# Sending the tenth weight chunk directly behind the ninth, in a hybrid decoder step with a mixture of 32 experts

## The reference, cut to what matters

```python
def decoder_layer(x, start, past_k, past_v, past_u, w):
    ...
    x = x + merged @ w['w_out']
    hn = rms_norm(x, w['norm_ffn_g']).reshape(B * S, D_MODEL)
    x = x + hier_moe(hn, ...).reshape(B, S, D_MODEL)

def hier_moe(h, ...):
    # top-1 of 4 groups, then top-2 of its 8 experts for every token
    ...
    def expert_block(args):
        xb, e = args
        return (jax.nn.silu(xb @ w_gate[e]) * (xb @ w_up[e])) @ w_down[e]
```

## Time and profile before

| | |
|---|---|
| median of three runs | 1030.26 us (1027.77 to 1032.42) |
| the profiled execution's own time | 1030.08 us |
| its span, first to last instruction | 1028.2 us |
| TensorE busy | 903.1 us (88%) |
| DVE, ACT, GpSimd busy | 365.2, 224.2, 85.4 us |
| moved by the DMA engines | 258.46 MB, mean 251 GB/s |
| DMA rate from about 540 us to about 1000 us | 385 to 413 GB/s |

### The profile page before, as it was taken

The page is one execution under the profiler, slowest core; times in us unless marked ns, Lnnn a source line. Parts: engine busy times, 40 slices in busy tenths (PEclk is TensorE's granted clock), DMA queues, the critical chain, the costliest instruction groups (busy, mean ns, idle before and its releaser), DMA issues.

```text
span 1028.2 us, 11181 instructions
## 1 busy us (share of the span) xinstructions
PE 903.1 (88%) x4299; PEld 507.0 (49%) x4299; DVE 365.2 (36%) x806; ACT 224.2 (22%) x570; POOL 85.4 (8%) x88
## 2 busy tenths in 40 slices
PE   6899799999899999999969999797777778887884
PEld 5454577777678888855533333233232323232331
DVE  4588568767343345533334111111011111111110
ACT  3432354254632100022211111001000000000010
POOL 0100000000000000000011211011111111010111
PEclk9999899999999999999969999899999999989998
DMA  9621212111112227088389999999999999999991
GB/s 316 202 82 71 93 42 81 51 42 58 66 42 82 83 82 263 15 346 339 144 301 400 395 388 393 390 411 397 400 401 403 410 398 413 403 413 396 405 393 44
DMA packets 33327, 258.46 MB, mean 251 GB/s; under 512 B 9000, under 2 KB 12328, under 8 KB 17768
## 3 DMA queue, kind: packets, MB, share of 16 engines
q1 hardware_dynamic: 27376, 245.45, 60.0%
q0 software_dynamic: 5904, 12.37, 4.6%
HBM read 252.46 MB, written 14.58 MB: 260 GB/s over the span
## 4 chain that ended last, share of the span: by engine, by line
PE 56%; DMA 26%; DVE 8%; issue 4%; ACT 4%; another core or an unknown queue 1%; SPq 1%; POOL 0%; POOLq 0%; DVEq 0%; ACTq 0%
DMA arena<-in_w_gu 19%; PE ps L1731 19%; PE ps L2004 12%; PE ps L2023 7%; PE ps L1670 6%; PE ps L1888 5%; DMA arena<-in_w_ed 5%; DMA arena<-in_x 2%; PE ps L1993 2%; DVE arena L1297 1%; ACT arena L833 1%; DVE a_stat L1323 1%; DVE arena L1320 1%; ACT arena L845 1%; PE ps L1747 1%
## 5 line engine op out<-in xcount | busy, mean ns | idle before, releaser
L1731 PE MATMUL ps<-arena 128*128 128x272 f32 x1120 | 269.4, 397 | 13.4 <-ACT arena L733 5.8
L2004 PE MATMUL ps<-arena 128*64 128x512 f32 x512 | 235.2, 608 | 20.7 <-DMA arena<-in_w_gu 20.4
L1731 PEld LDWEIGHTS ps<-arena 128*128 128x128 f32 x1120 | 209.9, 191 | 65.0 <-ACT arena L733 11.5
L2005 PE MATMUL ps<-arena 128*64 128x512 f32 x512 | 235.4, 609 | 0.0
L2023 PE MATMUL ps<-arena 128*64 128x512 f32 x512 | 132.9, 666 | 56.6 <-issue 44.0
L733 ACT ACTIVATE arena<-ps 128x272 f32<-128x272 f32 (+5 forms) x172 | 77.3, 457 | 399.0 <-PE ps L2023 172.8
L2004 PEld LDWEIGHTS ps<-arena 128*64 128x64 f32 x512 | 67.5, 139 | 158.9 <-issue 125.5
L1529 DVE SCALAR_TENSOR_TENSOR arena<-ps,list_w,arena 64x512 f32<-64x512 f32 x32 | 23.7, 742 | 290.1 <-ACT arena L998 290.1
L2023 PEld LDWEIGHTS ps<-arena 128*64 128x64 f32 x512 | 43.4, 151 | 143.2 <-issue 134.5
L1670 PE MATMUL ps<-arena 128*128 128x512 f32 (+1 forms) x192 | 75.2, 549 | 8.8 <-DMA arena<-in_w_kv 7.4
L692 POOL DMA_INDIRECT out_y<-arena,list_i x32 | 45.6, 1426 | 403.4 <-PE ps L1993 346.1
(11 more groups left out here) (224 smaller groups left out, 691.3 us busy)
## 6 DMA issues: line engine op xcount, KB each, us to landing
arena<-in_w_gu SPq DMA_DIRECT2D x64, 2048.0 KB, 48.7
arena<-in_w_ed SPq DMA_DIRECT2D x32, 2048.0 KB, 50.9
arena<-in_w_pair SPq DMA_DIRECT2D x20, 1024.0 KB, 4.8
arena<-in_x SPq DMA_DIRECT2D x8, 512.0 KB, 8.6
arena<-in_w_q SPq DMA_DIRECT2D x2, 2048.0 KB, 15.4
arena<-in_w_out SPq DMA_DIRECT2D x2, 2048.0 KB, 12.5
arena<-in_x_T SPq DMA_DIRECT2D x4, 512.0 KB, 9.3
out_y<-arena SPq DMA_DIRECT2D x4, 512.0 KB, 5.9
```

The lines of the kernel that those rows point to most:

```text
L1731: ins = mm(out, w[:, k, :], tokens[:, k, :], start=k == 0 and q in "127", stop=k == 3, skip_group_check=q not in "127")
L2004: mm(ps[0:C, 2 + s, :], xT[s][:, j, :], w[:, jj, 0, :], start=j == 0, stop=j == JX - 1)
L2005: ins = mm(ps[64:64 + C, 2 + s, :], xT[s][:, j, :], w[:, jj, 1, :], start=j == 0, stop=j == JX - 1)
```

## The change

SP no longer waits for the first expert's gathered rows before it sends chunk 9.

```diff
             t = ORDER[NT - 1]
             sp.dma_start(hn_rows[t * P:t * P + ROWS[t], :], xn[(NT - 1) % 2][0:ROWS[t], :]).then_inc(hn_last, 16)
             load_chunk(EARLY + 1)
-            sp.wait_ge(x_full[0], 16)
             load_chunk(EARLY + 2)
```

## The result

The changed kernel took 1032.10 us (median of 20 runs, 1029.47 to 1035.39), the kernel before, run beside it, 1028.78 us (20 runs, 1025.93 to 1033.18). The ratio is 1.0037, with a 95% interval of 1.0025 to 1.0048: slower by 3.8 us (2.6 to 4.9); the two medians lie 3.3 us apart. The forecast was a shift of 4.0 us and, as most likely, a change within 0.5%. The forecast of the time itself, 1034.1 us, came out 2.0 us lower, mostly because the kernel before takes 1028.78 us over 20 runs and not the 1030.26 of the first three. The profiled span is 1032.3 us, where 1032.2 was forecast: this is closer than the parts of the sum deserve.

The account below looks back on a forecast made before the run. The prediction took the gapless stream of weight chunks from chunk 10 on to set the pace, with TensorE waiting for it. Its terms, 0 + 0 + 4.0 + 0 + 0 = +4.0 us on 1030.08, gave 1034.1 us, range 1029.5 to 1037.5.

Parts of the forecast that it names:

- Steps 1 and 2: SP's queue at chunks 9 and 10: losing 10.1 us of waiting gains nothing, and chunk 10 finds no freer engines; 0.
- Step 3: Expert 0's gather meets chunk 9 on the DMA engines and lands when that chunk does; +4.0 us.
- Step 4: First eight matmul pairs on TensorE: the clock rises 4.6 us behind the first pair again, block keeps its length; 0.
- Step 5: Gathers of experts 2 and 3: they no longer meet chunk 9, but are first needed after 538 us; 0.
- Step 6: Stream from chunk 10 on: issued at 536.6, all behind it moves by the same 4.0 us, nothing given back.
- A: Expert 0's gather passes beside chunk 9, a shift of 0.6 to 1.2 us, time about 1031; chance 0.20.
- B: Expert 0's gather waits longer than one chunk, 9.1 to 11.1 us, time 1035.3 to 1037.3; chance 0.15.
- C: First eight matmul pairs at full clock, gather not held up, chunk 10 finds empty engines; -2.3 us, 1027.8; chance 0.04.
- D: No change: TensorE's idle time later in the stream makes up the shift, time 1030.1; chance 0.06.

Follow-up runs that it names:

- e5: The kernel before, but chunk 9 waits until TensorE has turned experts 0 and 1; ratio to the kernel before 1.0007.
- e1: The kernel before, but chunk 9 goes in two halves, the first directly behind chunk 8, the second after the first expert's rows land; ratio 1.0023.
- e4b: The changed kernel with 14 added matmuls (128x448, results never used) in TensorE's pauses ahead of the experts; ratio to the kernel before 1.0032.
- e7: The changed kernel run once more, unaltered, for a second profile; ratio to the kernel before 1.0049.
- e9: The changed kernel with 11 added matmuls (128x128) in TensorE's pause between the first expert's product and turning its hidden values; ratio to the kernel before 1.0026.
- e2: The changed kernel, but chunk 9 is sent as four transfers with rows of 4 KB instead of one with 16 KB; ratio to the kernel before 1.0036.
- e8: The kernel before with 4, 2 and 3 added matmuls (128x256, results never used) sized to TensorE's pauses ahead of the experts; ratio 0.9992.
- e4: The kernel before with 14 added matmuls (128x448, results never used) in TensorE's pauses ahead of the experts; ratio 1.0039.
- e3: The changed kernel, but chunk 8 goes ahead of the last tile's output and normalised rows, chunk 9 directly behind those rows; ratio to the kernel before 1.0034.
- e8b: The changed kernel with 4, 2 and 11 added matmuls (128x256, results never used) in TensorE's pauses ahead of the experts; ratio to the kernel before 1.0024.

## Why the prediction was right

**Steps 1 and 2** (nothing gained by the missing wait) held. SP's 10.1 us of waiting are gone, and the DMA engines stand nearly empty from 527 to 536 instead. In the changed kernel chunk 10 finds them empty and takes 7.6 us, no less than the 7.3 of before, so it had lost nothing to chunk 9. From the other side e5 agrees, where chunk 9 sent 1.7 us later begins to get in its way (8.8 us). One reading was too strong: in the microsecond ahead of the 0.28 the share is 0.93, mostly the gathers of experts 2 and 3.

**Step 3** (the gather lands when the chunk ahead of it does) is the cause, and the right one: the gather's packets do not start for 3 us, e1 halves the bytes and the extra delay goes from 4.7 to 1.9 us, and in e4b, where the gather comes behind most of the chunk, 1.1 us is left of it and the cost is gone. Its size was set at 4.0 us, and it measured 4.7 and 4.6. I had chunk 9 landing 5.4 us behind chunk 8; it landed about 7.2 us behind (513.12 + 8.3 = 521.4 and 514.06 + 14.6 = 528.7), and the gather 0.3 us before it:

```profile
arena<-in_w_gu SPq DMA_DIRECT2D x1, 2048.0 KB, 8.3
...
arena<-in_w_gu SPq DMA_DIRECT2D x1, 2048.0 KB, 14.6
...
arena<-hn_rows,list_i POOLq DMA_INDIRECT x1, 8.6
```

The term was 4.7 us for the chunk at the full rate of 442 GB/s, and something for the gathers. The rows show where it was short: with the gathers' packets among the chunk's the engines were busy for 0.96 and 0.70 of the last two microseconds and carried only 291 and 181 GB/s, and next to nothing moved after 527, though the landings came at 528.4 and 528.7. The row of expert 4's gather, 9.1 us with a fresh chunk ahead, was a slightly better price (measured 8.6, forecast 7.9).

**Step 4** (the clock rises as long after the first pair as before) was off by 0.8 us in this profile. The clock rose at 533.4, 2.9 us behind the first pair and not 4.6, and the eight pairs took 5.1 us instead of 5.9. So chunk 10 moved by 4.7 - 0.8 = 3.9 us, as measured. This is not a fixed gain of the change. In the other kernels that have it and no work added ahead, the pairs took 5.2 (e7), 5.6 (e9) and 5.8 us (e2). The clock's rise moves from one execution to the next, and 0 was as fair a forecast as could be made.

**Step 5** (the gathers of experts 2 and 3) held: they landed after 3.2 us (median of the two), where expert 2's had taken 6.8, and nothing in the chain waited for them.

**Step 6** (everything behind chunk 10 moves as one, since the stream has no gap) was too simple. Between chunks 10 and 12 the stream still hangs on TensorE's pace, and the second fall of the clock cost 1.7 us there, of which 1.2 and 0.3 us are left at chunk 93 in the two profiles (472.6 and 471.8 us from chunk 10's issue to its landing, before 471.5). In e2, without that fall, it is 471.6: there everything behind chunk 10 does move as one. What brings the fall isn't shown. The change alone doesn't, as e2 and e8 show.

The terms then sum to 4.7 - 0.8 + 1.2 = 5.1 us for the first profile of the changed kernel against the one of before, less the 0.9 us by which its first stages were shorter: 4.2 us between the landings of chunk 93, and 4.1 between the spans. That the profiled span was forecast to 0.1 us is luck, since the two terms of the clock and the shorter first stages belong to this one execution. That the ratio's 3.8 us is near 4.0 is partly luck too: the gather's delay was set 0.7 us too short, and in the profiles the shorter eight pairs gave back 0.1 to 0.8 us of it.

**The rivals.** A, a gather that passes beside the chunk at a cost of 0.6 to 1.2 us, would have landed it after 4.5 to 5.1 us and is refuted by 8.6, 8.5 and 7.9. By the Trainium skill (DMA: Bandwidth & Descriptors, section "Issuing engines are not separate DMA queues") such transfers run on the same 16 engines and interleave. The trace agrees only from 523 on, when packets of both queues stand in the same microsecond; before that, for 3 us behind the gather's issue, it has none of the gather's. B, a wait of 9.1 to 11.1 us, was just missed by the gather (8.6). C is dealt with at e4 and e8. D fell with the result.

No version here beat the kernel before beyond its interval. The wait that the change removes sits at a point where chunk 9 is out of the gather's way and still in time for chunk 10.

## What to carry to other kernels

A bulk transfer that nobody needs soon is not free because its queue is idle: ask which small transfer will be issued while it moves, and who waits for that one. A wait in front of a prefetch may be there to keep a path clear, and its price must be read at the small transfer's landing, not at the queue's idle time. When a bulk transfer is moved ahead of others instead, everything behind it on its own queue has to be priced too, as e3 shows.

## What the runs showed of the hardware that was not expected

- A gather of 0.26 MB issued by GpSimd behind 2 MB of SP's landed after 8.5 to 9.0 us, behind 1 MB after 5.8, and with little or nothing in its way after 3.5 to 3.9. In the changed kernel none of its packets moved in the first 3 us behind its issue. Cutting the 2 MB into 4 transfers with rows of 4 KB in place of 16 KB made 7.9 of 8.6.
- A write of 0.5 MB on SP's queue took 7.8 us to land behind one chunk of 2 MB, and 2.9 to 3.6 us without it.
- In nine executions in which TensorE's granted clock rose from 1.2 to 2.4 GHz within the same eight pairs of matmuls, with no work added ahead of them, these took from 5.1 to 6.3 us. In five of the thirteen profiles (both of the changed kernel, e3, e8 and e8b) the clock fell again behind the next pause; the start of the stage alone does not decide it, since e2 starts late and keeps it and e8 starts as before and loses it. In e8b the clock fell to 1.2 GHz near 526.7, although TensorE had been filled with work up to 524.1 and again from 525.7.
